# Four changes of order in a two-layer hybrid encoder kernel: a load released without its wait, a cast, a DMA-add and the last blocks of a product moved

## The reference

```
h = rmsnorm(x) ; p = h @ W_in                  # u, v (gMLP), q, k, v, gate (GLA), two ranks for the decay
out_A = gelu(u) * (W_s @ layernorm(gelu(v)) + b)      # 4 heads, chunks of 128
out_B = rmsnorm(gla_forward + gla_backward) * silu(gate)
x = x + concat(out_A, out_B) @ W_out
z = dwconv3(rmsnorm(x) @ W_up)                 # W_up: 1024 x 5632
x = x + (silu(z_gate) * z_val) @ W_down        # W_down: 2816 x 1024
```

## Time and profile before

| what | us |
|---|---|
| median of three executions | 1063.7 |
| the profiled execution | 1060.73 |
| its span in the trace | 1058.9 |
| TensorE busy | 1048.7 |
| GpSimd busy | 791.4 |
| VectorE busy | 649.6 |
| ScalarE busy | 637.2 |

### The profile page before, as it was taken

One profiled execution on the slowest core, in us unless ns is written; L12 is line 12 of the kernel. 1 busy time (PEld: TensorE's weight loads), 2 busy tenths in 40 slices (PEclk: granted clock), 3 DMA queues, 4 the chain that ended last, 5 costly groups with the idle time before them and its releaser, 6 DMA issues.

```text
span 1058.9 us, 19238 instructions
## 1 busy us (share of the span) xinstructions
PE 1048.7 (99%) x6876; PEld 944.4 (89%) x6876; DVE 649.6 (61%) x946; ACT 637.2 (60%) x902; POOL 791.4 (75%) x442
## 2 busy tenths in 40 slices
PE   9999999999999999999999999999999999999997
PEld 7788888998999989998878888889989998899987
DVE  4889974676157721776649799547652766146654
ACT  8977557775367623775569674667644774266641
POOL 5788448996999767994558763699969995699940
PEclk9999999999999999999999999999999999999999
DMA  8575346786898757972516742659759975789502
GB/s 307 154 157 165 107 139 160 210 189 179 228 234 191 219 145 173 212 173 80 186 54 167 161 164 97 191 108 256 206 156 238 218 177 163 179 201 236 141 21 80
DMA packets 52661, 180.68 MB, mean 171 GB/s; under 512 B 5840, under 2 KB 8656, under 8 KB 52304
## 3 DMA queue, kind: packets, MB, share of 16 engines
q1 hardware_dynamic: 36720, 121.71, 35.0%
q0 software_dynamic: 15136, 56.63, 28.9%
q10 hardware_dynamic: 704, 1.07, 0.3%
HBM read 152.12 MB, written 2.10 MB: 146 GB/s over the span
## 4 chain that ended last, share of the span: by engine, by line
PE 81%; POOL 9%; DVE 3%; DMA 2%; issue 2%; ACT 1%; SPq 0%; DVEq 0%; ACTq 0%; POOLq 0%
PE acc L2286 12%; PE acc L2289 12%; PE acc L2288 12%; PE acc L1975 9%; PE acc L1977 9%; PE acc L1976 9%; POOL w_lo L655 6%; PE acc L2123 2%; PE acc L2124 2%; PE acc L2125 2%; PE acc L2108 1%; PE acc L2107 1%; PE acc L2106 1%; DMA second_s<-arena 1%; PE sides L2194 1%
## 5 line engine op out<-in xcount | busy, mean ns | idle before, releaser
L655 POOL TENSOR_TENSOR w_lo<-w_raw,w_hi 128x1024 fp32r<-128x1024 f32 x152 | 388.8, 2662 | 117.4 <-ACT w_hi L951 93.8
L2286 PE MATMUL acc<-xg_hi,w_hi 128*128 128x256 f32 x688 | 195.5, 284 | 0.0
L2288 PE MATMUL acc<-xg_lo,w_hi 128*128 128x256 f32 x688 | 194.7, 283 | 0.0
L2289 PE MATMUL acc<-xg_hi,w_lo 128*128 128x256 f32 x688 | 194.7, 283 | 0.0
L1975 PE MATMUL acc<-feat_hi,w_hi 128*128 128x512 f32 (+1 forms) x484 | 185.4, 383 | 0.0
L1976 PE MATMUL acc<-feat_lo,w_hi 128*128 128x512 f32 (+1 forms) x484 | 185.0, 382 | 0.0
L1977 PE MATMUL acc<-feat_hi,w_lo 128*128 128x512 f32 (+1 forms) x484 | 184.9, 382 | 0.0
L951 ACT ACTIVATE w_hi<-w_raw 128x1024 fp32r<-128x1024 f32 x128 | 133.5, 1054 | 58.6 <-PE acc L1977 23.9
L2286 PE MATMUL acc<-t_hi,w_hi 128*128 128x256 f32 x528 | 149.9, 284 | 1.5 <-POOL w_lo L655 1.1
L2288 PE MATMUL acc<-t_lo,w_hi 128*128 128x256 f32 x528 | 149.4, 283 | 0.0
L2289 PE MATMUL acc<-t_hi,w_lo 128*128 128x256 f32 x528 | 149.4, 283 | 0.0
(11 more groups left out here) (230 smaller groups left out, 2192.9 us busy)
## 6 DMA issues: line engine op xcount, KB each, us to landing
w_raw<-slabs SPq DMA_DIRECT2D x128, 512.0 KB, 4.5
arena<-slabs SPq DMA_DIRECT2D x32, 512.0 KB, 4.6
mixer_sb<-slabs SPq DMA_DIRECT2D x26, 512.0 KB, 5.6
arena<-slabs POOLq DMA_DIRECT2D x24, 512.0 KB, 6.1
w_raw<-slabs POOLq DMA_DIRECT2D x20, 512.0 KB, 6.1
w_raw<-slabs SPq DMA_DIRECT2D x6, 1024.0 KB, 5.9
third_raw<-slabs POOLq DMA_DIRECT2D x6, 1024.0 KB, 8.6
second_s<-slabs SPq DMA_DIRECT2D x12, 512.0 KB, 5.8
```

Source lines behind the costliest of these rows:

```text
L655: pool.tensor_tensor(lo, source, hi.bitcast(F32), ALU.subtract).then_inc(lo_done, counted(unit))
L2286: pe.matmul(out, wh, xh, start=(first and k == 0 and r == 0), stop=False, skip_group_check=True)
L2288: pe.matmul(out, wh, xl, start=False, stop=False, skip_group_check=True)
L2289: last = pe.matmul(out, wl, xh, start=False, stop=(k == KP - 1), skip_group_check=True)
```

## The change

It does four things in each of the two layers:

- SP no longer waits for `third_added` before the load of block 3.
- POOL issues `add_s1` of quad 2 behind the low part of quad 1's S1, and no longer ahead of it.
- DVE makes `m1_lo` ahead of `add_va(0)` and `add_va(1)`, and no longer behind them.
- PE, in part 0, does the last two blocks first for accumulators 0 to 2 and then both for accumulator 3; before, it did block 4 for all four and then block 5 for all four.

```diff
@@ SP, load_wide
                 low_of(L, wide(S4_, 1))
-                sp.wait_ge(third_added, 48 * L + 48)
                 sp.dma_start(two(wide_raw[1]), wide_block(L, 3)).then_inc(wide_loaded, 16)
@@ POOL, low_quad
                 low_of_quad(L, q, S1_)
-                if following and q > 1:
+                if following:
                     add_s1(L, q + 1)
                 low_of_quad(L, q, A11_)
@@ POOL, after quad 0
                 add_s2(L, 1)
-                add_s1(L, 2)
@@ DVE
+                dve.wait_ge(t1_hi_done, L * 2 * KP + KP)
+                dve.tensor_tensor(m1_lo[:, :], m1_raw, m1_hi[:, :].bitcast(F32), ALU.subtract).then_inc(t1_ready, KP)
                 add_va(0, 2, kept, L * 8)
                 add_va(1, 2, kept, L * 8)
-                dve.wait_ge(t1_hi_done, L * 2 * KP + KP)
-                dve.tensor_tensor(m1_lo[:, :], m1_raw, m1_hi[:, :].bitcast(F32), ALU.subtract).then_inc(t1_ready, KP)
@@ PE, down_products
-                    order += [(k, j) for k in range(early, blocks) for j in range(RING if d == 0 else 3)]
-                    if d:
-                        order += [(k, 3) for k in range(blocks)]
+                    order += [(k, j) for k in range(early, blocks) for j in range(3)]
+                    order += [(k, 3) for k in range(early if d == 0 else 0, blocks)]
```

## The result

The changed kernel takes 1075.01 us (median of four executions, 1072.76 to 1076.96) against 1062.66 us before in the same comparison (four executions, 1060.73 to 1064.02): ratio 1.0117, 95% interval 1.0101 to 1.0135. It is slower by 12.4 us, where 5.1 were forecast and 1073.5 was the upper end of the range. The profiled execution took 1073.27 us; its span is 1071.4 us, 12.5 more than before.

The account below looks back on a forecast made before the run. TensorE, busy for 1048.7 of 1058.9 us, was taken as the bound, so reordering could only make it wait: 1.2 (POOL) + 1.4 (PE) + 2.5 (wide stage) = 5.1 us, giving 1068.8 from a median of 1063.7; range 1064.6 to 1073.5.

Parts of the forecast that it names:

- The load without its wait (SP): Wide stage: freed load delays `wide_s1`'s add 2.3 us; less 1.04 slack, TensorE waits 1.26 per layer, 2.5 in all.
- First come, first served: DMA queues at the wide stage: the transfer that comes first keeps the engines, here the load, with the `u` slab after.
- All loads go first: Rival, wide stage: load and two `u` slabs delay the add 4.44 us, TensorE waits 3.4 per layer; 1073.1 us, chance 0.15.
- The rule on queues: DMA engines take turns between queues packet by packet; the add would land some 2 us later, less the free share.
- POOL's add of quad 2's S1: Quad 1: the moved issue delays the low part of S2 by 0.61 us per layer, 1.2 us in all.
- The last blocks (PE): End of part 0: TensorE waits 0.68 us per layer for tile 5's low part, 1.4 us in all.
- m1_lo ahead of add_va (DVE): Ahead of S4: `m1_lo` still ends at 80.3, adds at 81.6, S4 0.5 us late; contained in the load's 1.26.
- (1): Sign: PE waits ahead of quad 1's S2 near 1.0 us for 0.38, twice.
- (2): Sign: a new PE wait for `feat_lo` of 0.6 to 0.7 us at tile 5 on accumulator 0, twice.
- (3): Sign: `add_va` ends near 81.6 and PE's S4 comes later by 0.5 us.
- (4): Sign: `wide_s1`'s add lands in 10 to 11 us for 8.4; PE waits for POOL's S1 low part by 0.8 or so.

Follow-up runs that it names:

- load_only: Kernel before, with block 3's load freed of its wait but the first `u` slab behind it waiting for the add's end: 1068.08 us, ratio 1.0051.
- sp_only: Kernel before with only SP's wait ahead of the load of block 3 taken out: 1074.25 us, ratio 1.009.
- load_after_start: Kernel before, with block 3's load waiting for S3's first low part instead of the add's end: 1069.25 us, ratio 1.0051.
- slabs_only: Kernel before, with the first two `u` slabs loaded ahead of block 3's load, which keeps its wait: 1061.79 us, ratio 0.9977.
- pool_only: Kernel before with only POOL's add of quad 2's S1 moved: 1063.71 us, ratio 0.9997.
- pe_only: Kernel before with only the order of PE's last blocks of part 0 changed: 1064.67 us, ratio 1.0012.
- dve_only: Kernel before with only `m1_lo` put ahead of `add_va` on DVE: 1065.09 us, ratio 1.0005.
- all_but_sp: Changed kernel with SP's wait put back, so POOL's, DVE's and PE's edits remain: 1065.64 us, ratio 1.0011 against the kernel before.
- load_late_b: Repeat of load_after_start, against the kernel before: 1071.03 us, ratio 1.0074.
- before_a: Kernel before, unchanged, run again for a second trace: 1067.14 us.
- start_between: load_after_start plus VectorE's select_scores(2) and (3) moved ahead of the two 128x512 operations of layernorm(1): 1062.95 us, ratio 0.9996 against the kernel before.

## Why the prediction was wrong, step by step

- **The load without its wait (SP): the step that failed.** The prediction took "1.86 and a third of 1.29, together 2.3 us" for the add's delay, and so a wait of 1.26 us per layer. The delay was 5.1 us (landing 13.5 for 8.4), and the waits were 3.63 and 3.52. The direction and the place were right; the delay, a term of the sum, was mis-sized, in three parts. First, 2.58 us for the load was its time in full flow; with its slow start it held the engines for 3.7 us (92.3% of 84:88). Second, 0.72 us were taken off as a free share of 84:86. Most of that share lies ahead of the add's first packets at 84.5, and once under way the add fills the engines (109.6% of 86:88 in the trace of before), so there was little to give back. load_only shows the two together: 3.4 us and not 1.86. Third, a `u` slab was counted by a third, 0.43 us; sp_only shows 1.6 more with the slabs than load_only without (1.2 in layer 2). "First come, first served" was seen, and load_after_start and slabs_only bear it out for what is issued once the add is at work.
- **The rival that came closest.** "All loads go first" has a delay of 4.44 us and 3.4 us per layer. Its 3.4 looks like the waits of 3.5 and 3.6, but that is luck in part. The rival means both edits of the wide stage together, and together they cost about 4.2 and 3.7 us. The delay of 5.1 was 0.7 larger than its 4.44, and in layer 1 the 0.6 us by which S4 came late hid as much of it from the wait. It had 0.15 of the chances.
- **The bound that was missing.** Even that rival ended at 1073.1. It lacked the fall of the granted clock behind a wait of 3.4 us, 1.4 us in layer 2 of this execution and about 1.5 in each layer of sp_only. No row of before shows TensorE stand still that long, but the upper end should have left room for it. Waits and clock together are 8.6 of the 12.5 us in the trace after; timed alone (sp_only, 1.009) the line costs 9.6 us, with an interval of 6.4 to 12.8.
- **The rule on queues.** By the turns between queues that the Trainium skill describes ("DMA: Bandwidth & Descriptors", section "Queues, rings and completion order") the add would have landed some 2 us late. The trace disagrees for the first four microseconds (92.3% to 3.1%). It agrees once both are under way: at 90:94 the add moves 131 packets to the loads' 123, 67.2% to 33.7% by time. Which transfer's packets are at work first decides, and that goes by their first packets, 1.0 us behind the issue for the load and 1.9 for the add, and not by 0.2 us of issue time.
- **POOL's add of quad 2's S1.** Forecast 1.2 us. In the trace after, quad 1 costs 0.34 and 0.74 more than before, 1.1 in all: right in size for the sum, but more of it falls ahead of A12 than ahead of S2, where the prediction had all of it. In pool_only it was 0.35 and 0.3, half of the forecast, so the sum's agreement is luck in part.
- **The last blocks (PE).** Forecast 0.68 per layer, read in the trace after 0.66 and 0.65; pe_only's time (1.0012, interval from 0.9995) can't confirm it.
- **m1_lo ahead of add_va (DVE).** Forecast: `m1_lo` ends at 80.3, the adds at 81.6, S4 0.5 late. Measured: 80.4, 81.6, S4 at 81.74 for 81.12 in layer 1, and about 0.2 us late in layer 2, so the second 0.5 was not there. The term rested on the lock between VectorE and GpSimd that the Trainium skill describes ("SBUF — State Buffer", section "SBUF: two separate sides"). `m1_lo` could start hardly sooner than before (77.99 for 78.00, 77.86 in dve_only), so these runs don't put the lock to the test at this place. Its 2.50 us agree with it, where half as wide an operation takes 0.69 with GpSimd standing still.
- **Signs.** (1) came at 0.49 for 0.38, weaker than the 1.0 forecast, with a new wait ahead of A12; (2) came as written, (3) in layer 1 only; (4) missed, 13.5 us for 10 to 11 and a wait of 3.5 for 0.8.
- **The base.** The profiled execution of before had no wait for the scores, where two other executions of the same kernel waited 1.0 and 1.9 us.

By the ratios sp_only's 9.6 us and all_but_sp's 1.2 us make 10.8 of the 12.4; the rest is within the intervals. How the three small edits divide their share in time stays open.

## What to carry to other kernels

A wait ahead of a prefetch that nobody needs yet may be there to keep the DMA engines for a transfer that somebody does need. Before it is taken away, count the whole time of every transfer that it held back, its slow start included, against the slack of the one that is wanted. If TensorE would then stand still for as long as it did here (3.4 to 4.2 us), leave room for a slow restart: it cost about 1.5 us behind three of these four waits and nothing behind the fourth. When several engines feed one another closely, look at what runs beside what: VectorE's layer norm took 2.6 us while GpSimd stood still, 8.5 in the kernel before and 13 with the late load, and the selection that TensorE needed was cheap to put ahead of its last two operations.

## What the runs showed of the hardware

- An add of 1 MB by GpSimd's queue lands in 8.3 to 8.6 us with no load beside it (once, in layer 2 of pe_only, in 9.4), and in 13.4 to 13.6 with 2 MB of loads from SP's queue, of which the first was issued 0.2 us behind it. When the load follows 3.8 us later, it lands in 8.9 to 9.1, and once, in layer 2 of load_late_b, in 10.4.
- The load's first packets began 1.0 us behind its issue (after, layer 1), the add's 1.9 us behind its own (before, layer 1). The first ones were slow, about 1 us each for the load where later ones took 0.16.
- TensorE's granted clock fell to about 0.5 for some 3 us behind waits of 1.85 (before_a), 3.28 (load_late_b), 3.36 (after, layer 2), 4.05 (load_after_start), 4.20 and 4.24 us (sp_only). It did not fall behind one of 3.48 (after, layer 1), nor behind those of 2.5 (load_only) and 1.83 (load_late_b). So in these traces the length of the wait alone doesn't tell.
- VectorE's operations in `layernorm(1)`, beside GpSimd's low parts: one of 128x512 0.69 us while GpSimd stood still and up to 2.78 us beside it; four scalings of 128x128 1.11 us and up to 9.13 us beside it (start_between).
